# Norm, gate and merge of the sequence per chunk, two first projection tiles slice by slice, inverted blocks interleaved with their transpose

## The chip, the cores and the metric

The kernel runs on one core of a Trainium2 chip. The metric is the device time of one execution in microseconds. The core has five engines with queues of their own: TensorE (PE, matrix products, with weight loads listed as PEld), VectorE (DVE), ScalarE (ACT), GpSimd (POOL, hardly used here) and SyncE (SP, which only issues transfers here). ScalarE issues transfers too (ACTq in the trace), and while it does, it computes nothing.

## What is computed

Two layers of a hybrid decoder, for a prompt of 256 tokens and 8 sample tokens, 264 in all, with a model width of 1024. Each layer has three sublayers: a feed-forward half step, the mixing, and a second feed-forward half step. Cut to what matters:

```python
x = sub_out(x, swiglu(sub_in(x, 0), ffn_up[0], ffn_down[0]), 0, 0.5)
h = sub_in(x, 1)
pa, pb, pg = split_cols(h @ w_in, [A_COLS, B_COLS, 2 * D_MODEL])
ya = rwkv7_branch(pa, ...)            # sequential state update, 16 heads of 64
yb = gdn_branch(pb, ...)              # gated DeltaNet, 8 heads of 128, chunks of 64 tokens
g_a, g_b = jnp.split(jax.nn.sigmoid(pg), 2, axis=-1)
x = sub_out(x, (g_a * ya + g_b * yb) @ w_out, 1, 1.0)
x = sub_out(x, swiglu(sub_in(x, 2), ffn_up[1], ffn_down[1]), 2, 0.5)
...
# gdn_branch, per chunk of 64 tokens
tinv = triangular_solve(eye + L, eye)                 # one 64x64 inverse per head and chunk
v_new = u_c - w_c @ S;  o = q_c @ S + a_c @ v_new;  S = S * exp(gl_c) + k_c.T @ v_new
...
o = o * rsqrt(mean(o * o, axis=-1) + 1e-6) * norm_w   # per head: over its 128 columns
o = o * silu(z)
```

The shift, scale and gate of each sublayer come from a conditioning vector by a product with w_ada.

## The kernel before

**Tiles and the weight stream.** Activations are kept feature-major, 128 partitions by 8 slices by 264 tokens. A weight tile is 128 output columns by 8 slices, 512 KB in fp32. SyncE loads the tiles, in the order of a plan that is written at the start (a list of keys), into a ring of five slots. ScalarE casts each tile to fp32r (`w_hi`, L718), VectorE makes the rest (`ring_r`, L726), and TensorE multiplies each slice three times: high by high, high by low, low by high (`linear`, L860), 24 matmuls a tile. A helper `ahead` has both make a tile two tiles before TensorE uses it. Conditioning tiles (`w_ada`) are in the same plan. They are used in pieces of four matmuls (`ada_piece`); during the mixing they all go through one slot of the ring, the fifth.

**Entries.** The first projection tile of a sublayer waits slice by slice for its activation (`entering`, `h_ready`), which ScalarE and VectorE make one slice after another.

**Mixing.** It has 76 turns (`TURNS`), in each of which `dense(t)` multiplies one tile of w_in. Every other part of the mixing hangs on turn numbers at the top of the file (L56 to L63), and the same turn loop is written for each engine, so the order on a queue is the order of this loop. The triangular inverses are made three times a layer (`run` 0, 1 for the RWKV branch, 2 for the gated DeltaNet) for 16 units of 128 rows at a time: `gather` (8 transfers from SBUF to DRAM, L563) and `fetch` bring the 16x16 diagonal blocks side by side, `solve` inverts them on VectorE, `store` writes the result and its transpose (L578), `clear` zeroes the target on ScalarE (L608, L609, L611), `scatter` issues 16 transfers of 16 KB from ScalarE that lay the blocks on the diagonals (L620), and `invert` joins the blocks to 32 and 64 by four steps of 64 or 128 small matmuls (L639, L647, L652), with VectorE between them. `invert` waits for all transfers of `scatter`; in the other direction the scatter waits for the clear.

**Tail.** After the last turn comes the gated DeltaNet over four chunks: on TensorE `attend(c)` and the state, on VectorE the new state and values. The output of a chunk lies in PSUM bank 4 and ScalarE copies it to `y` (L1774). Sample steps and reads of the sample states (`sample_reads`) are laid between the chunks. Only after the last chunk come the norm (ScalarE squares a head, TensorE sums it with `ones_all`, ScalarE makes logarithm and exponential, L1378 and L1380), six VectorE operations for the head (L2322 to L2335), and this for eight heads one after another. The out projection waits for all eight (`merged`). Behind the merge ScalarE issues loads of sample states.

Of the kernel before, what the change touches and what calls it, by code (L numbers as in the profile page):

```python
# [19 lines left out]
P = 128  # L20
DEPTH, D = 2, 1024
NT = D // P
# [34 lines left out]
PREP0, CONV0, SEQ0, MOUT, LAST_AT = 5, 28, 40, 52, 53  # L57
UNIT0, ROWS0, HEAD0, GN0, SAMP0, SILU0 = 53, 53, 56, 61, 64, 70
# [3 lines left out]
GATHER0, FETCH0, SOLVE0, STORE0 = (18, 30, 65), (19, 31, 66), (20, 32, 67), (22, 34, 69)  # L62
CLEAR0, SCATTER0, INV0 = (29, 34, 67), (30, 35, 70), (31, 36, 71)  # L63
# [72 lines left out]
def weight_plan():  # L136
# [3 lines left out]
    for l in range(DEPTH):  # L140
# [14 lines left out]
        for t in range(TURNS):  # L155
            plan.append((l, *TILES[t]))
# [36 lines left out]
def build(nc, I, O):  # L193
    ctx = ExitStack()
    with ctx:
# [108 lines left out]
        def g_bv4(hf, cp, g):  # L304
# [5 lines left out]
        t_blocks = nc.dram_tensor("t_blocks", [2, P, B16, B16], F32, kind="Internal").ap()  # L310
        solve_bufs = [[qk[:, 21 + n, 3:3 + NPR] for n in range(3)] + [qk[:, 20, 3:3 + NPR]]] * 2
        solve_bufs += [[pa[:, NT + n, 0:NPR] for n in range(4)]]
        inv_sets = [(g_lt if n == 2 else prod_b[:, UNITS * n:UNITS * (n + 1), C:2 * C], part(big, inv_t_at[n], UNITS, C),
                     part(big, inv_t_at[n] + 1024, UNITS, C), part(big, inv_x_at[n], UNITS, C)) for n in range(3)]
# [10 lines left out]
        p_tmp = part(big, NT * T, 4, T)  # L325
# [212 lines left out]

        INV_PE = 5
# [32 lines left out]
        def store(act, run):  # L572

            act.wait_ge(solved.sem, solved.at(run + 1))
            if run:
                act.wait_ge(block_out.sem, block_out.at(18 * run))
            for n in range(2):
                act.dma_start(t_blocks[n, :, :, :], square(solve_bufs[run][1 + n])).then_inc(block_out.sem, block_out.one())  # L578

        def solve(dve, run, half):  # L580

            got, t_blk, tt_blk, prod = solve_bufs[run]
            got, t_m = square(got), square(t_blk)
# [5 lines left out]
            if half == 0:  # L589
                if run == 1:  # L590
                    dve.wait_ge(block_out.sem, block_out.at(18))
                dve.wait_ge(block_in.sem, block_in.at(9 * (run + 1)))
                after(dve.tensor_scalar(t_m, got.rearrange("p s t -> p t s"), -1.0, None, ALU.mult))
                dve.memset(t_blk[:, 0:NPR:B16 + 1], 1.0)
# [6 lines left out]
            if half == 1:  # L601
                dve.tensor_copy(square(tt_blk), t_m.rearrange("p t s -> p s t")).then_inc(solved.sem, solved.one())

        def clear(act, run):

            lt, t_b, tt_b, x_b = inv_sets[run]
            zero = bm(ident64[:, :], UNITS)
            act.mul(t_b, zero, 0.0)  # L608
            i = act.mul(tt_b, zero, 0.0)  # L609
            if run != 1:  # L610
                i = act.mul(x_b, zero, 0.0)  # L611
            i.then_inc(inv_z.sem, inv_z.one())

        def scatter(act, run):

            act.wait_ge(inv_z.sem, inv_z.at(run + 1))
            act.wait_ge(block_out.sem, block_out.at(18 * run + 2))
            for n, into in enumerate(inv_sets[run][1:3]):
                for rows, cols, part_of in blocks():
                    act.dma_start(into[rows, :, cols], t_blocks[n, part_of, :, :].rearrange("u s t -> s u t")).then_inc(block_out.sem, block_out.one())  # L620

        def invert(pe, run, s):

            lt, t_b, tt_b, x_b = inv_sets[run]
            n = 4 + s // 2
            if s == 0:

                pe.wait_ge(block_out.sem, block_out.at(18 * (run + 1)))
# [7 lines left out]
            if s % 2 == 0:  # L636
                for u in range(UNITS):
                    for hf in HALVES:
                        i = pe.matmul(banks[2][hf, u * 32:(u + 1) * 32].rearrange("p (a t) -> p a t", t=1 << n), lt[hf, u, :],  # L639
                                      unit_cols(t_b[hf, u, :], n, 0), start=True, stop=True)  # L640
# [3 lines left out]
            if n < 5:  # L644
                for u in range(UNITS):
                    for hf in HALVES:
                        i = pe.matmul(banks[4][hf, u * 32:(u + 1) * 32].rearrange("p (a t) -> p a t", t=1 << n), tt_b[hf, u, :],  # L647
# [1755 lines left out]
```

## Time and profile before

| what | us |
|---|---|
| median of three runs | 2300.95 (2300.72 to 2302.95) |
| profiled execution | 2309.99 |
| its span in the trace | 2308.3 |
| TensorE busy | 2076.7 (90%) |
| VectorE busy | 1269.5 (55%) |
| ScalarE busy | 958.1 (42%) |
| mean DMA rate | 153 GB/s |

Durations come from the one profiled execution, which was a little slower than the median run. "Busy" leaves out the issuing of transfers, so ScalarE is occupied longer than its 42%. PEclk is the granted clock of TensorE as a share of full speed. A wait is idle time of an engine just before an instruction, put down to the instruction that ended it.

### The profile page before, as it was taken

Reading aid. Unit: us, or ns where it says so; the run is one execution under the profiler, and the core shown is the slowest. Engines: PE = TensorE matmul, PEld = TensorE weight load, DVE = VectorE, ACT = ScalarE, POOL = GpSimd, SP = SyncE. Lnnn points to the kernel's source line nnn. Section 1 sums busy time; section 2 is a strip of 40 time slices with the busy share of each in tenths; the row PEclk is TensorE's granted clock in tenths of the full one; section 3 lists DMA queues with packets and bytes.
Section 4 is the critical chain, followed back from the end, with each engine's and each line's share of the span. In section 5 each row is a group of like instructions: output and inputs, shape, how many; then the busy total and the mean of one; then the engine's idle time right before and its main releaser. Section 6 shows DMA issues by size and latency. Waiting matters only on the chain.

```text
span 2308.3 us, 44992 instructions
## 1 busy us (share of the span) xinstructions
PE 2076.7 (90%) x19116; PEld 1863.6 (81%) x19116; DVE 1269.5 (55%) x2227; ACT 958.1 (42%) x1890; POOL 4.8 (0%) x30
## 2 busy tenths in 40 slices
PE   6999898989989896899989998988798988779997
PEld 4899777878878875788989996877797877569997
DVE  3454445654466256577556644464554744658863
ACT  3343553434475304423454445333345642153343
POOL 0000000000000000000000000000000000000000
PEclk7999999989999867899999999889899987689999
DMA  7877555555555615587646664444344444237863
GB/s 244 227 223 209 153 168 164 147 143 142 145 140 148 159 46 128 151 240 228 192 124 181 177 176 135 119 122 111 89 117 125 110 116 121 71 101 211 231 195 95
DMA packets 593718, 353.35 MB, mean 153 GB/s; under 512 B 57140, under 2 KB 554326, under 8 KB 591966
## 3 DMA queue, kind: packets, MB, share of 16 engines
q1 hardware_dynamic: 489344, 302.23, 45.9%
q10 hardware_dynamic: 104174, 48.25, 8.7%
q8 instruction: 151, 2.47, 0.5%
q14 instruction: 49, 0.40, 0.1%
HBM read 332.27 MB, written 18.50 MB: 152 GB/s over the span
## 4 chain that ended last, share of the span: by engine, by line
PE 73%; DVE 9%; DMA 6%; ACT 5%; ACTq 4%; issue 3%; SPq 0%; DVEq 0%
PE bank L858 70%; DMA ring<-in_w_ada 3%; ACTq L620 2%; DVE ring_r L726 1%; DMA ring<-in_ffn_up 1%; PE bank L639 1%; ACT w_hi_r L718 1%; DVE big L1838 1%; DVE far L1838 1%; PE bank L652 1%; DMA far<-t_blocks 1%; DVE y L1841 1%; DVE h L1838 1%; DVE y L1838 1%; PE bank L647 1%
## 5 line engine op out<-in xcount | busy, mean ns | idle before, releaser
L858 PE MATMUL bank<-big_r,w_hi_r 128*128 128x264 f32 x4160 | 1091.4, 297 | 49.7 <-DVE h_r L1838 37.6
L858 PE MATMUL bank<-big_r,ring_r 128*128 128x264 f32 (+1 forms) x3456 | 1004.1, 291 | 0.0
L858 PEld LDWEIGHTS bank<-big_r,w_hi_r 128*128 128x128 f32 x4160 | 758.1, 194 | 126.8 <-issue 94.9
L858 PE MATMUL bank<-h_r,w_hi_r 128*128 128x264 f32 x2752 | 807.7, 293 | 0.0
L726 DVE TENSOR_TENSOR ring_r<-ring,w_hi_r 128x1024 fp32r<-128x1024 f32 (+2 forms) x440 | 524.2, 1195 | 464.9 <-ACT w_hi_r L718 461.2
L858 PEld LDWEIGHTS bank<-big_r,ring_r 128*128 128x128 f32 (+1 forms) x3456 | 673.7, 195 | 1.0
L718 ACT CAST w_hi_r<-ring 128x1024 fp32r<-128x1024 f32 (+2 forms) x440 | 452.8, 1030 | 480.5 <-PE bank L858 291.7
L858 PEld LDWEIGHTS bank<-h_r,w_hi_r 128*128 128x128 f32 x2752 | 541.4, 197 | 1.1
L858 PE MATMUL bank<-big,far 64*64 64x64 f32 (+2 forms) x1440 | 159.1, 266 | 0.0
L858 PEld LDWEIGHTS bank<-big,far 64*64 64x64 f32 (+1 forms) x1440 | 124.5, 144 | 7.6 <-issue 7.1
L858 PE MATMUL bank<-ring,c 128*32 128x256 f32 x1152 | 96.4, 415 | 20.9 <-DMA ring<-in_w_ada 15.6
L1838 DVE TENSOR_TENSOR big<-big,bank 128x264 f32<-128x264 f32 (+3 forms) x144 | 66.4, 468 | 72.2 <-PE bank L858 60.1
L858 PE MATMUL bank<-big 128*64 128x64 f32 (+5 forms) x608 | 81.6, 299 | 16.0 <-DVE big L1838 14.4
L858 PE MATMUL bank<-far 64*64 64x64 f32 (+2 forms) x928 | 89.1, 255 | 1.1 <-ACT far L1497 1.1
L858 PEld LDWEIGHTS bank<-big 128*64 128x64 f32 (+2 forms) x608 | 60.8, 181 | 34.0 <-DVE big L1838 19.1
L858 PEld LDWEIGHTS bank<-far 64*64 64x64 f32 (+2 forms) x928 | 64.8, 145 | 15.7 <-issue 12.7
L1841 DVE SCALAR_TENSOR_TENSOR rs<-big,pcol,rs 128x256 f32<-128x256 f32 x78 | 37.8, 485 | 58.2 <-ACT rs L1542 56.0
L639 PE MATMUL bank<-far 64*64 64x32 f32 x768 | 34.1, 256 | 37.5 <-DMA far<-t_blocks 37.5
L858 PE MATMUL bank<-far,big 64*64 64x64 f32 (+1 forms) x576 | 67.7, 255 | 0.0
L639 PEld LDWEIGHTS bank<-far 64*64 64x64 f32 x768 | 32.6, 178 | 39.6 <-DMA far<-t_blocks 38.8
L858 PEld LDWEIGHTS bank<-ring,c 128*32 128x32 f32 x1152 | 24.5, 112 | 47.4 <-DMA ring<-in_w_ada 23.4
L858 PEld LDWEIGHTS bank<-far,big 64*64 64x64 f32 (+1 forms) x576 | 57.5, 162 | 6.0
(288 smaller groups left out, 1981.5 us busy)
## 6 DMA issues: line engine op xcount, KB each, us to landing
ring<-in_ffn_up SPq DMA_DIRECT2D x176, 512.0 KB, 4.3
ring<-in_w_in SPq DMA_DIRECT2D x148, 512.0 KB, 3.8
ring<-in_w_ada SPq DMA_DIRECT2D x144, 512.0 KB, 4.1
ring<-in_ffn_down SPq DMA_DIRECT2D x64, 512.0 KB, 3.8
far<-in_state_gdn_ssm ACTq DMA_DIRECT2D x28, 512.0 KB, 5.4
ring<-in_ffn_down SPq DMA_DIRECT2D x32, 384.0 KB, 3.2
ring<-in_w_out SPq DMA_DIRECT2D x16, 512.0 KB, 3.8
out_sample_gdn_ssm<-far ACTq DMA_DIRECT2D x16, 512.0 KB, 4.2
```

Source lines behind the costliest of these rows:

```text
L620: act.dma_start(into[rows, :, cols], t_blocks[n, part_of, :, :].rearrange("u s t -> s u t")).then_inc(block_out.sem, block_out.one())
L639: i = pe.matmul(banks[2][hf, u * 32:(u + 1) * 32].rearrange("p (a t) -> p a t", t=1 << n), lt[hf, u, :], unit_cols(t_b[hf, u, :], n, 0), s ...
L647: i = pe.matmul(banks[4][hf, u * 32:(u + 1) * 32].rearrange("p (a t) -> p a t", t=1 << n), tt_b[hf, u, :], unit_cols(x_b[hf, u, :], n, 0), ...
L652: i = pe.matmul(banks[3][hf, u * 32:(u + 1) * 32].rearrange("p (a t) -> p a t", t=1 << n), x_b[hf, u, :], unit_cols(tt_b[hf, u, :], n, 1), ...
L718: act.copy(w_hi[:, m % HI, 0:size], ring[:, slot[n], 0:size]).then_inc(hi_ready.sem, hi_ready.one())
L726: dve.tensor_tensor(ring_r[:, slot[n], 0:size], w, w_hi[:, m % HI, 0:size].bitcast(F32), ALU.subtract).then_inc(lo_ready.sem, lo_ready.one())
L858: return pe.matmul(out, lhsT, rhs, start=start, stop=stop)
L1838: return dve.tensor_tensor(out, a, b, op)
L1841: return dve.scalar_tensor_tensor(out, a, s, b, op0, op1)
```

## The change

There are three parts.

1. The inverted blocks and their transposes are held in one array whose last dimension is 2 (block value, transposed value). So there is one store and there are 8 scatters of 16x16x32 elements instead of 16 of 16x16x16, the clear is two operations, and the operands of `invert` are read at a step of two floats. The turn numbers move: there is one turn more between scatter and inversion, and what depends on the inverses (`SEQ0` and the constants behind it) comes two turns later.
2. `enter` multiplies the first two tiles of a sublayer's projection slice by slice together, at all six entries. In the mixing the plan has both tiles ahead of the first two conditioning tiles.
3. Norm, silu gate, branch gates and merge of the gated DeltaNet are made per chunk (64 tokens, all eight heads at once, 512 columns) during the chunk sequence, and the sample reads move ahead of the chunks. The branch gates and the conditioning operations move to the head of the tail.

```diff
-PREP0, CONV0, SEQ0, MOUT, LAST_AT = 5, 28, 40, 52, 53
-UNIT0, ROWS0, HEAD0, GN0, SAMP0, SILU0 = 53, 53, 56, 61, 64, 70
+PREP0, CONV0, SEQ0, MOUT, LAST_AT = 5, 28, 42, 54, 55
+UNIT0, ROWS0, HEAD0, GN0, SAMP0, SILU0 = 55, 55, 58, 63, 66, 72
-GATHER0, FETCH0, SOLVE0, STORE0 = (18, 30, 65), (19, 31, 66), (20, 32, 67), (22, 34, 69)
-CLEAR0, SCATTER0, INV0 = (29, 34, 67), (30, 35, 70), (31, 36, 71)
+GATHER0, FETCH0, SOLVE0, STORE0 = (18, 30, 66), (19, 31, 67), (20, 32, 68), (22, 34, 69)
+CLEAR0, SCATTER0, INV0 = (29, 35, 67), (30, 36, 70), (32, 38, 72)
...
         def scatter(act, run):
...
-            for n, into in enumerate(inv_sets[run][1:3]):
-                for rows, cols, part_of in blocks():
-                    act.dma_start(into[rows, :, cols], t_blocks[n, part_of, :, :].rearrange("u s t -> s u t")).then_inc(block_out.sem, block_out.one())
+            into = inv_sets[run][1].rearrange("p u t w -> p u (t w)")
+            for rows, cols, part_of in blocks():
+                act.dma_start(into[rows, :, 2 * cols.start:2 * cols.stop], t_blocks[part_of].rearrange("u s t w -> s u (t w)")).then_inc(block_out.sem, block_out.one())
...
+                    def enter(outs, keys, x_hi):
+
+                        both = [weights((l, *key)) for key in keys]
+                        for k in range(NT):
+                            pe.wait_ge(h_ready.sem, h_ready.next(pe))
+                            for out, (hi, lo) in zip(outs, both):
+                                mm(out, hi[:, k, :], x_hi[:, k, :], k == 0, False)
+                                mm(out, hi[:, k, :], h_lo[:, k, :], False, False)
+                                i = mm(out, lo[:, k, :], x_hi[:, k, :], False, k == NT - 1)
...
+                    def post_sum(c):
+
+                        pe.wait_ge(post_sq.sem, post_sq.at(c + 1))
...
+                        mm(bank, ones_all[:, :], square.rearrange("p n t -> p (n t)")).then_inc(post_ss.sem, post_ss.one())
...
                     for c in range(1, NC):
+                        first, *others = ((0, 1), (2, 3, 4), (5, 6, 7))[c - 1]
+                        sample_reads(first)
+                        post_sum(c - 1)
+                        for n in others:
+                            sample_reads(n)
...
+                    def post_square(c, bank):
...
+                        act.activation(post_t[c][1], src, ACT.Square).then_inc(post_sq.sem, post_sq.one())
+                        return act.copy(y[:, :, post_cols[c]], src)
...
+                    for c in range(NC + 1):
+                        post_cut(c)
...
+                    act.wait_ge(merged.sem, merged.at(NC + 1))
                     load_samples(samp_both, sa_in)
...
+                    def post(c):
+
+                        dve.wait_ge(post_rs.sem, post_rs.at(c + 1))
+                        yc = y[:, :, post_cols[c]]
+                        settle(stt(yc, yc, g_nw, post_t[c][0], ALU.mult, ALU.mult))
+                        settle(tt(yc, yc, zs[:, :, post_cols[c]]))
+                        tt(yc, yc, pa[:, 0:NT, post_cols[c]], ALU.add).then_inc(scaled.sem, scaled.one())
+
+                    def post_low(c):
+                        dve.wait_ge(cut_ready.sem, cut_ready.next(dve))
+                        tt(h_lo[:, :, post_cols[c]], y[:, :, post_cols[c]], hi_out[:, :, post_cols[c]].bitcast(F32), ALU.subtract).then_inc(merged.sem, merged.one())
```

On ScalarE, turn 30, the first run's scatter; `far` is the SBUF array that holds the target and `lt_blocks` the gather of the next run. Before:

```order
L1368 COPY modv<-bank7 128x36
L718 CAST w_hi_r<-ring 128x1024
L1486 COPY big<-bank0 128x264
L1487 COPY svx<-bank0 128x11
L620 DMA far<-t_blocks 16x16x16 x16
L563 DMA lt_blocks<-far 16x16x16 x8
L1547 ACTIVATE big<-svx 128x256
L1542 ACTIVATE rs<-big,pcol 128x256
L718 CAST w_hi_r<-ring 128x1024
```

The same place of the change:

```order
L1402 COPY modv<-bank7 128x36
L723 CAST w_hi_r<-ring 128x1024
L1520 COPY big<-bank0 128x264
L1521 COPY svx<-bank0 128x11
L625 DMA far<-t_blocks 16x16x32 x8
L570 DMA lt_blocks<-far 16x16x16 x8
L1581 ACTIVATE big<-svx 128x256
L1576 ACTIVATE rs<-big,pcol 128x256
L723 CAST w_hi_r<-ring 128x1024
```

The sequence around it is the same; the scatter is half as many transfers, each twice as large, and the gather still stands behind it.

On TensorE, the end of the first layer's tail, from the last chunk's output (bank 4) to the out projection (bank 0). Before, with the two remaining sample reads (`cva`), one bridge per sample step (bank 7), and the eight norm sums:

```order
L858 MATMUL bank4<-big 128x64
L858 MATMUL bank4<-far,big 128x64
L858 MATMUL bank2<-far,cva 16x128 x8
L858 MATMUL bank7<-ident64,svx 64x64 x2
L858 MATMUL bank2<-far,cva 16x128 x8
L858 MATMUL bank7<-big,centre 128x64
L858 MATMUL bank3<-ysel,far 128x32 x2
L858 MATMUL bank7<-rs,ones_half 128x64
L858 MATMUL bank4<-big,ones_all 128x264
L858 MATMUL bank5<-big,ones_all 128x264
...
L858 MATMUL bank0<-big_r,w_hi_r 128x264
```

The change:

```order
L863 MATMUL bank4<-big 128x64
L863 MATMUL bank4<-far,big 128x64
L863 MATMUL bank2<-ysel,far 128x32 x2
L863 MATMUL bank7<-ident64,svx 64x64 x2
L863 MATMUL bank3<-far,ones_all 128x512
L863 MATMUL bank7<-big,centre 128x64
L863 MATMUL bank1<-far,ones_all 128x64
L863 MATMUL bank7<-rs,ones_half 128x64
L863 MATMUL bank0<-big_r,w_hi_r 128x264
```

Both sample reads and eight sums have left this stretch; one sum of 512 columns and one of 64 are in it. The other three sums and the reads stand between the chunks.

On TensorE, the entry of the mixing in the first layer; bank 0 and bank 1 take the first two tiles, `ring,c32` is a conditioning piece. Before, one place ahead of the second tile and one behind it:

```order
L858 MATMUL bank0<-big_r,ring_r 128x264
L858 MATMUL bank7<-ring,c32 32x256 x4
L858 MATMUL bank1<-big_r,w_hi_r 128x264
L858 MATMUL bank1<-h_r,w_hi_r 128x264
...
L858 MATMUL bank1<-big_r,ring_r 128x264
L858 MATMUL bank7<-ring,c32 32x256 x4
L858 MATMUL bank0<-big_r,w_hi_r 128x264
```

The change, the last slice of both tiles and what follows:

```order
L863 MATMUL bank0<-big_r,ring_r 128x264
L863 MATMUL bank1<-big_r,w_hi_r 128x264
L863 MATMUL bank1<-h_r,w_hi_r 128x264
L863 MATMUL bank1<-big_r,ring_r 128x264
L863 MATMUL bank7<-ring,c32 32x256 x8
L863 MATMUL bank0<-big_r,w_hi_r 128x264
```

The tiles alternate by slice, and the two conditioning pieces, which had a whole tile between them, stand back to back.

## Rows read from the trace of the kernel before

**Rows 1.** The page, busy time and share of TensorE, weight loads and other engines.

```profile
PE 2076.7 (90%) x19116; PEld 1863.6 (81%) x19116; DVE 1269.5 (55%) x2227; ACT 958.1 (42%) x1890; POOL 4.8 (0%) x30
```

**Rows 2.** The waits of TensorE: us in total, times, longest us.

```profile
PE bank L858 <- DVE h_r L1838: 37.6, 8, 8.2
PE bank L639 <- DMA far<-t_blocks: 37.5, 6, 9.9
...
PE bank L858 <- ACT big L1813: 25.2, 16, 1.9
```

**Rows 3.** Timeline of ScalarE, first inversion: start, us, engine, line, what, count.

```profile
474.51 1.33 ACTq L620 DMA_DIRECT2D far<-t_blocks  x3
...
475.87 6.47 ACTq L620 DMA_DIRECT2D far<-t_blocks  x13
482.44 4.65 ACTq L563 DMA_DIRECT2D lt_blocks<-far  x8
```

**Rows 4.** Timeline of TensorE, first inversion, its steps 0 and 2.

```profile
484.14 3.62 PE L639 MATMUL bank<-far 64*64 64x32 f32 x64 [5.93 <-DMA far<-t_blocks]
...
500.59 2.06 PE L639 MATMUL bank<-far 64*64 64x32 f32 x64
```

**Rows 5.** Windows: length, busy (count) of PE, PEld, DVE, ACT, POOL, clock, DMA, GB/s.

```profile
484.10:490.10 6.00, 5.96 (x78) 5.08 (x79) 2.04 (x4) 2.67 (x7) 0.00 (x0) 0.50 0.28 46
788.50:868.60 80.10, 74.91 (x501) 62.65 (x501) 38.15 (x41) 7.18 (x12) 0.00 (x0) 0.72 0.35 86
...
898.40:928.40 30.00, 29.92 (x208) 29.05 (x208) 10.03 (x9) 14.22 (x33) 0.00 (x0) 0.90 0.71 193
```

**Rows 6.** Timeline of ScalarE and of TensorE, second inversion of layer 1.

```profile
1646.97 1.94 ACTq L620 DMA_DIRECT2D far<-t_blocks  x2
...
1657.33 3.63 PE L639 MATMUL bank<-far 64*64 64x32 f32 x64 [9.92 <-DMA far<-t_blocks]
```

**Rows 7.** Timeline of ScalarE, end of the first layer's tail.

```profile
862.66 0.59 ACT L1774 COPY y<-bank 128x512 f32<-128x512 f32 x1 [19.23 <-PE bank L858]
...
875.15 0.48 ACT L1378 ACTIVATE big<-bank,epsc 128x264 f32<-128x264 f32 x1 [1.40 <-PE bank L858]
...
898.47 2.37 ACTq L1823 DMA_DIRECT2D far<-in_state_gdn_ssm  x3
```

**Rows 8.** Timeline of TensorE, end of the first layer's tail.

```profile
866.48 2.15 PE L858 MATMUL bank<-far,cva 128*16 128x128 f32 x16
...
873.80 1.25 PE L858 MATMUL bank<-big,ones_all 128*128 128x264 f32 x2 [1.85 <-ACT big L1813]
...
898.43 0.59 PE L858 MATMUL bank<-big_r,w_hi_r 128*128 128x264 f32 x1 [3.88 <-DVE h_r L1838]
```

**Rows 9.** Timeline of VectorE, head and end of the first layer's tail.

```profile
796.80 0.69 DVE L2216 COPY big<-bank 128x512 f32<-128x512 f32 x1 [8.99 <-PE bank L858]
...
870.93 2.35 DVE L1838 TENSOR_TENSOR far<-far,delta 128x1024 f32<-128x1024 f32 x2
...
876.85 0.49 DVE L1841 SCALAR_TENSOR_TENSOR y<-y,pcol,far 128x264 f32<-128x264 f32 x1
```

**Rows 10.** Timeline of TensorE, entry of the first mixing.

```profile
284.04 0.56 PE L858 MATMUL bank<-big_r,w_hi_r 128*128 128x264 f32 x1 [4.32 <-DVE h_r L1838]
284.39 0.42 PE L858 MATMUL bank<-h_r,w_hi_r 128*128 128x264 f32 x1
284.61 0.42 PE L858 MATMUL bank<-big_r,ring_r 128*128 128x264 f32 x1
...
290.32 0.64 PE L858 MATMUL bank<-ring,c 128*32 128x256 f32 x8
290.89 0.39 PE L858 MATMUL bank<-big_r,w_hi_r 128*128 128x264 f32 x1
...
295.75 0.64 PE L858 MATMUL bank<-ring,c 128*32 128x256 f32 x8 [1.69 <-DMA ring<-in_w_ada]
```

More of the change, by code:

```diff
@@ L324, in build @@
         vnx = part(big, gt + 1024, 2, NS, HD_B)
-        p_tmp = part(big, NT * T, 4, T)
+        post_cols = [slice(c * C, (c + 1) * C) for c in range(NC)] + [slice(NPR, T)]
+        post_t = [(part(big, WORK, NT, C), part(big, WORK + 512, NT, C))] * NC + [(part(big, WORK + 1024, NT, NS), part(big, WORK + 1088, NT, NS))]
         gs_kept = [part(big, ZG + 1024 * n, NS, HD_B) for n in range(3)]
@@ L537, in level_bank, with pair_cols @@
             return banks[bank][:, :].rearrange("p (u a t) -> p u a t", u=UNITS, t=1 << n)
+        def pair_cols(both, n, w, side, u=None):
+            cols = "p u (a h t) -> p u a h t" if n == 4 else "p u (h a t) -> p u a h t"
+            v = both[:, :, :, w].rearrange(cols, h=2, t=B16)[:, :, :, side, :]
+            return v if u is None else v[:, u]
         INV_PE = 5
@@ L575, in store @@
             if run:
-                act.wait_ge(block_out.sem, block_out.at(18 * run))
-            for n in range(2):
-                act.dma_start(t_blocks[n, :, :, :], square(solve_bufs[run][1 + n])).then_inc(block_out.sem, block_out.one())
+                act.wait_ge(block_out.sem, block_out.at(9 * run))
+            act.dma_start(t_blocks[:, :, :, :], solve_bufs[run][1]).then_inc(block_out.sem, block_out.one())
         def solve(dve, run, half):
-            got, t_blk, tt_blk, prod = solve_bufs[run]
-            got, t_m = square(got), square(t_blk)
+            got, both, prod = solve_bufs[run]
+            got, t_m = square(got), both[:, :, :, 0]
             def after(i):
@@ L601, in solve @@
             if half == 1:
-                dve.tensor_copy(square(tt_blk), t_m.rearrange("p t s -> p s t")).then_inc(solved.sem, solved.one())
+                dve.tensor_copy(both[:, :, :, 1], t_m.rearrange("p t s -> p s t")).then_inc(solved.sem, solved.one())
         def clear(act, run):
[L606 to L609, printed above, removed]
+            lt, both, x_b = inv_sets[run]
+            zero = bm(ident64[:, :], 2 * UNITS)
+            i = act.mul(both.rearrange("p u (a t) w -> p (u a) (t w)", a=2), zero, 0.0)
             if run != 1:
-                i = act.mul(x_b, zero, 0.0)
+                i = act.mul(x_b, bm(ident64[:, :], UNITS), 0.0)
             i.then_inc(inv_z.sem, inv_z.one())
@@ L858, in mm, with weights @@
                         return pe.matmul(out, lhsT, rhs, start=start, stop=stop)
-                    def linear(out, key, x_hi, x_lo, start=True, stop=True, entering=False):
-                        key = (l, *key)
+                    def weights(key):
                         m, n = split_no[key], where[key]
@@ L865, in linear @@
                         pe.wait_ge(lo_ready.sem, lo_ready.nth(m + 1))
[L866 to L867 removed]
+                        return (w_hi[:, m % HI, 0:kt * cols].rearrange("p (k n) -> p k n", k=kt),
+                                ring_r[:, slot[n], 0:kt * cols].rearrange("p (k n) -> p k n", k=kt))
+                    def linear(out, key, x_hi, x_lo, start=True, stop=True):
+                        hi, lo = weights((l, *key))
+                        kt = tile_size(*key)[0]
                         for k in range(kt):
[L869 to L870 removed]
                             mm(out, hi[:, k, :], x_hi[:, k, :], start and k == 0, False)
@@ L975, in dense @@
                         if k < 2:
-                            pe.wait_ge(out_taken.sem, out_taken.at(NT))
+                            if k == 0:
+                                pe.wait_ge(out_taken.sem, out_taken.at(NT))
+                                enter([banks[g][:, 0:T] for g in range(2)], TILES[0:2], hi_in)
+                            return
                         elif k - 2 < A_TILES:
@@ L1708, in _ @@
                         for run in range(3):
-                            if t == GATHER0[run]:
+                            if t == GATHER0[run] and run < 2:
                                 gather(act, run)
@@ L1712, in _ @@
                                 fetch(act, run)
-                            if t == STORE0[run]:
+                            if t == STORE0[run] and run < 2:
                                 store(act, run)
```

229 lines of the change are left out of this document (116 added, 113 removed).

## The prediction

> **What bounds the kernel now.** I read the page first: TensorE has work in 2076.7 of 2308.3 us [rows 1], a share of 90%. So time comes back where TensorE waits, or where it runs at the lower clock after a wait. VectorE and ScalarE matter only where TensorE waits for them. The list of TensorE's waits comes next [rows 2]: 37.6 us for the low part of an activation (eight places, two of them at the out projections), 37.5 us in six waits for the scattered inverse blocks, 25.2 us in 16 waits for the squares of the post norm. The change touches all three.
>
> The six waits. There are three inversions in a layer. ScalarE issues 16 scatters for one, about 0.50 us each (13 in 6.47) [rows 3]. In the first, the last issue ends at 482.34 and TensorE starts at 484.14, after 5.93 us of nothing; the 64 small matmuls behind it take 3.62 us, and the same kind takes 2.06 us at 500.59 [rows 4]. The granted clock in the six us after the wait is 0.50 of full, the 1.2 GHz level [rows 5]. So a wait costs more than itself. The longest wait is 9.92 us, in layer 1 [rows 6].
>
> The post norm. Behind the last chunk's copy at 862.66 [rows 7] TensorE has eight squares to sum, each behind a 1.5 us wait on ScalarE, and the out projection starts only at 898.43, 3.88 us after it had nothing more [rows 8]. Between them stand, head by head, the square, the sum, a logarithm, an exponential and six VectorE operations, such as the one of 0.49 us [rows 9], all in a row.
>
> **The change, part by part.** The sum is against the profiled execution: 2309.99 us, of which the trace spans 2308.3. That run is 9.04 us over the median of 2300.95, and I carry this difference along.
>
> *Inversion.* Removed: 8 of 16 scatter issues (4.0 us of ScalarE's queue), one of two stores, one of three clears. Added: one more turn between scatter and first inversion matmul (30 to 32, 36 to 38, 70 to 72; before one turn less in each). For the first run: the scatter starts at 474.51 or a little later, eight issues with the work between them end near 479.2, and 2.3 us later (484.14 less the start of the last issue, 481.86) the blocks lie near 481.1. TensorE stood ready at 484.14 - 5.93 = 478.21. The turn that now comes first is a projection tile, 24 matmuls in 3.17 us (290.89 to 295.75 - 1.69 [rows 10]) and in most turns a conditioning piece of 0.64: 3.6 us and more, so 481.8 or later. No wait is left, but the margin is 0.7 us only. For the longest wait TensorE was ready at 1657.33 - 9.92 = 1647.41 and the scatter began at 1646.97 [rows 6]: with eight issues it lands about 7.1 us on, TensorE comes after 4.5, and some 2.5 us stay. I take 35.0 of 37.5 us as gone. Clock: five of the six blocks return 3.62 - 2.06 = 1.56, which is 7.8. The tile behind each block has its matmuls 0.22 apart where it takes 0.13 at full clock [rows 10]; over 24 that is 2.2 if the clock stays low for the whole tile, and I take 1.5, times five 7.5. Together 50.3. Against it, what moves in: the turn that TensorE now computes meets casts and copies that still queue behind eight scatter and, in the first run, eight gather issues (4.65 us [rows 3]) on ScalarE. Before, ScalarE's next work could begin at 482.44 + 4.65 = 487.1; with four us less it is 483.1, its cast and VectorE's low part end near 486.2, and TensorE needs them at about 484. I give it 2.3 us in all, since it can show in two of the six. **Minus 48.** Bounds: if the moved turn is worth nothing, the waits shrink by the 4.0 us of issues alone, 24 and some clock, minus 27. If all waits go and the small stalls of the neighbouring turns with them, minus 58.
>
> *Operands two words apart.* T and its transpose now alternate, so moving data and one kind of weights are read at a step of two floats. No row shows this. From below nothing. From above, that each group of 64 falls from 2.06 to the 3.62 us [rows 4] of half speed: 5 groups in a run, 30 in all, 1.56 more each, 47 us. The pace of the group follows TensorE's clock now (3.62 against 2.06), so the array bounds it, and a slower read counts only beyond that; I take 0. The Trainium skill speaks to it in SBUF — State Buffer, section Door 1: The DMA port swizzle, in its note on cachelines: a 16-byte line wants at least two hits, so fp32 at a step of two, two hits a line, should run at full rate; by that the sum stays, by the half-speed bound it would be 2276. No row here shows it either way, and the sum doesn't use it.
>
> *Tail.* Per layer, 898.43 - 862.66 = 35.8 us now. In it remain: the square of the last chunk, 0.6 (as the copy, 128x512 [rows 7]); the sum on TensorE, 2.4 at the rate of 1.25 for 264 columns [rows 8]; logarithm and exponential, the first 0.48 for 264 columns [rows 7], so about 1.25 for both at 512; three VectorE operations at some 0.75 (0.69 for a copy of 512 [rows 9]), 2.2; the sample step and its merge, 2.3; the cut and the low parts, 3.1 (four at 0.7 and a small one). That is 11.9, and 0.4 for hand-overs: 12.3. The norms of chunks 0 to 2 go under the chunk sequence, where VectorE has 38.15 busy of 80.1 us [rows 5]; if that cover were gone they would cost about 2.2 us of VectorE a chunk. What is not hidden is TensorE's part: three sums of 512 columns, 1.5 each between the two clock levels, 4.5; and two sample reads of 2.15 [rows 8], which stood behind the last chunk and now stand ahead, 4.3. So 35.8 - 12.3 - 4.5 - 4.3 = 14.7, times two 29.4. The large gate operations move to the head of the tail, where VectorE idles 8.99 us before the first copy of u [rows 9]; two of 2.35 us (2048 elements [rows 9]) and four small ones fit. **Minus 28**, with 0.7 a layer for hand-overs inside the sequence. Bounds: minus 22, where each sum takes the full 2.4 us and a hand-over, and minus 34, where the sums and reads hide in waits that TensorE has there anyway. Four loads of 512 KB more now go out after the merge, ahead of the cast of the third out tile: before 3 took 2.37 us [rows 7], seven take 5.5. The cast comes at about 904, TensorE needs it after two tiles, 48 matmuls at 0.22, 909. Hidden; next to be late would be the tile loads themselves.
>
> *Entries.* Six entries now run two tiles slice by slice. Now tile 0 takes from 284.04 to 290.32, 6.28 us or 0.79 a slice, where its matmuls need 3 x 0.22 = 0.66; tile 0, the piece and tile 1 end at 294.06, 10.0 us after the start [rows 10]. Interleaved: the clock rose after six us, so 27 of 48 matmuls at 0.22, then 21 at 0.13, 8.7 us, against 9.4 without the piece: 0.7 gained at most, and in the four feed-forward entries the third tile's cast and low part wait behind the table load, so I put 0.5 each there, minus 2. In the two mixing entries both conditioning pieces now follow the two tiles, and they share one slot of the ring: the second load starts only when the first piece is read. It came 295.75 - 290.96 = 4.8 us after the first piece, of which 1.69 were a wait [rows 10]. Now nothing lies between them and two tile loads go ahead of it: 4.8 to 6.0 of waiting, 3.1 to 4.3 more, less 0.7. **Plus 6** for two, **plus 4** with the others. Bounds plus 1 and plus 8.
>
> Sum: -48 - 28 + 4 = -72. Profiled execution 2238, median 2300.95 - 72 = 2229. With the bounds: -27 - 22 + 8 = -41 to -58 - 34 + 1 = -91.
>
> **Rivals.**
> (a) The waits of the inversion only change hands. TensorE gets to the moved turn and stands there for ScalarE, which is still issuing, or the half clock stays since it falls for other gaps nearby. For it: the 0.7 us margin above, and ScalarE's queue of issues, which is blocked for 4.65 us more by the gathers behind the first [rows 3]. Against it: 4 us of issue are truly gone. Then -16 - 28 + 4: 2261, or little above.
> (b) The other side: strided reads are slow. It decides at 72 / 30 = 2.4 us more for each group of 64, 2.06 to 4.5. At three times the duration, 4.1 x 30 = 124, the result is 2353. Against it: that the array's clock sets the pace now. With the half-speed price of 47 it is 2276, still faster.
> (c) Transfers collide after the merge. Near 898 to 928 the DMA share is 0.71 at 193 GB/s, 5.8 MB in 30 us [rows 5]; 2 MB more need 10 us at this rate, and if half of it holds up the tiles: +5 a layer, 2239.
> (d) Everything goes at its upper bound: 2210.
> (e) The change does nothing measurable: the waits reappear in full and the tail's gain is eaten by the entries and the sums inside the sequence. It needs two independent failures.
>
> **Chances.** The forecast with its bounds, (c) within it: 0.73. (a) 0.10. (d) and beyond 0.08. (b) 0.05, of which 0.03 slower, and 0.02 for a slowdown of another kind. (e) 0.02. The range reaches from just under (d) to (a): 2207 to 2262. This kernel's measurement tells no change apart from 0.2%, 4.6 us. Faster 0.93, same 0.02, slower 0.05.
>
> **What would show it.** The six waits at the inversion's first matmuls should be near zero in the list of waits, their blocks of 64 at 2.1 us; if the blocks take 3.6 after no wait, operands are slow. ScalarE's scatters should be 48, the last issue some 4 us after the first. From the last chunk's square to the first out-projection matmul 12 to 13 us. The conditioning waits should grow by 6 us or so at the two mixing entries. The prediction is wrong if TensorE's waits for ScalarE's casts or VectorE's low parts grow by 15 us or more, if the chunk sequence (80.1 us now) grows by more than 12, or if the out projection stalls on its tiles.

## The result and the profile after

The changed kernel takes 2271.5 us (median of four runs, 2266.79 to 2278.63), the kernel before 2301.95 in the same comparison. The ratio is 0.9869, with a 95% interval of 0.9842 to 0.9897: 24 to 36 us faster, where 72 were forecast and 39 was the least that the range held.

The page of the changed kernel: span, busy time, and the chain that ended last by line.

```profile
span 2270.3 us, 44806 instructions
...
PE 2062.6 (91%) x19104; PEld 1854.5 (82%) x19104; DVE 1257.5 (55%) x2161; ACT 954.2 (42%) x1872; POOL 4.8 (0%) x30
...
PE bank L863 71%; DMA ring<-in_w_ada 3%; DVE ring_r L731 2%; DVE far L1888 1%; ACT w_hi_r L723 1%; DVE big L1888 1%; PE bank L657 1%; PE bank L644 1%; ACTq L1873 1%; DMA ring<-in_ffn_up 1%; ACTq L625 1%; ACTq L570 1%; DVE big L1891 1%; DVE far L1891 1%; PE bank L652 0%
```

Its waits of TensorE, in us in total, times, longest:

```profile
PE bank L863 <- DVE h_r L1888: 42.2, 8, 8.2
...
PE bank L863 <- DMA ring<-in_w_ada: 33.4, 21, 6.3
PE bank L863 <- DVE ring_r L731: 19.2, 7, 7.3
...
PE bank L644 <- DMA far<-t_blocks: 5.6, 2, 2.8
```

Against [rows 2]: the wait for scattered blocks fell from 37.5 to 5.6 us, the one for the squares of the post norm (25.2) is gone. Two others grew. Conditioning tiles cost 15.6 us in 16 waits before and cost 33.4 in 21 now; low parts of weight tiles (`ring_r`) cost 5.4 us before and 19.2 now. These two, 31.6 us together, are most of what is missing.

The largest of the first kind is at the entries of the mixing; one is in each layer. It answers to the last of [rows 10]. Timeline of TensorE:

```profile
299.16 1.08 PE L863 MATMUL bank<-ring,c 128*32 128x256 f32 x8 [6.17 <-DMA ring<-in_w_ada]
```

The second kind is in the out projection. Timeline of ScalarE behind the last chunk of layer 0, answering to [rows 7]:

```profile
867.73 0.60 ACT L1814 ACTIVATE far<-bank 128x512 f32<-128x512 f32 x1 [16.58 <-PE bank L863]
...
871.13 0.69 ACT L1412 ACTIVATE far<-bank,epsc 128x512 f32<-128x512 f32 x1 [1.78 <-PE bank L863]
871.85 0.63 ACT L1414 ACTIVATE far<-far 128x512 f32<-128x512 f32 x1
...
879.57 2.42 ACTq L1690 DMA_DIRECT2D far<-in_state_rwkv_wkv  x4
882.02 9.91 ACTq L1873 DMA_DIRECT2D far<-in_state_gdn_ssm  x3
892.03 1.04 ACT L723 CAST w_hi_r<-ring 128x1024 fp32r<-128x1024 f32 x1 [14.76 <-issue]
```

And TensorE in the same stretch, answering to [rows 8]:

```profile
869.02 2.07 PE L863 MATMUL bank<-far,ones_all 128*128 128x512 f32 x2
...
879.59 0.59 PE L863 MATMUL bank<-big_r,w_hi_r 128*128 128x264 f32 x1 [6.26 <-DVE h_r L1888]
...
894.39 0.59 PE L863 MATMUL bank<-big_r,w_hi_r 128*128 128x264 f32 x1 [7.30 <-DVE ring_r L731]
```

From the last square to the out projection it is 11.9 us (forecast 12.3). But the third out tile comes at 894.39. ScalarE makes its cast only at 892.03, because it issues seven loads of 512 KB first: four take 2.42 us, the three behind them 9.91, where three had taken 2.37 [rows 7]. The kernel before issued its four of these loads 29 us earlier than the three, at 869.46. It has such a slow issue too, at the head of the first tail, where ScalarE issues seven loads of 512 KB in a row; six take 5.7 us, the seventh 7.26:

```profile
791.36 3.08 ACTq L1762 DMA_DIRECT2D far<-in_state_gdn_ssm  x2
794.48 7.26 ACTq L1762 DMA_DIRECT2D big<-in_state_gdn_ssm  x1
```

### The profile page after: what moved, and what is told of

It reads as the page before. It is cut to its first block, busy times and chain, and to the rows that moved or that the text cites. A ratio compares the mean times of both kernels' runs of the same rounds, so it can differ in the third digit from the quotient of the medians.

```text
span 2270.3 us, 44806 instructions
## 1 busy us (share of the span) xinstructions
PE 2062.6 (91%) x19104; PEld 1854.5 (82%) x19104; DVE 1257.5 (55%) x2161; ACT 954.2 (42%) x1872; POOL 4.8 (0%) x30
## 4 chain that ended last, share of the span: by engine, by line
PE 74%; DVE 9%; DMA 6%; ACT 5%; ACTq 4%; issue 3%; SPq 0%; DVEq 0%
PE bank L863 71%; DMA ring<-in_w_ada 3%; DVE ring_r L731 2%; DVE far L1888 1%; ACT w_hi_r L723 1%; DVE big L1888 1%; PE bank L657 1%; PE bank L644 1%; ACTq L1873 1%; DMA ring<-in_ffn_up 1%; ACTq L625 1%; ACTq L570 1%; DVE big L1891 1%; DVE far L1891 1%; PE bank L652 0%
## 5 line engine op out<-in xcount | busy, mean ns | idle before, releaser
L863 PE MATMUL bank<-ring,c 128*32 128x256 f32 x1152 | 98.0, 420 | 36.7 <-DMA ring<-in_w_ada 33.4
L1888 DVE TENSOR_TENSOR big<-big,bank 128x264 f32<-128x264 f32 (+3 forms) x144 | 66.4, 468 | 87.0 <-PE bank L863 75.5
L1888 DVE TENSOR_TENSOR far<-bank,masks 128x512 f32<-128x512 f32 x32 | 20.6, 686 | 75.9 <-PE bank L863 75.9
L863 PE MATMUL bank<-ident,far 64*64 64x64 f32 (+1 forms) x608 | 60.4, 234 | 0.0
```

Source lines behind the costliest of these rows:

```text
L863: return pe.matmul(out, lhsT, rhs, start=start, stop=stop)
L1888: return dve.tensor_tensor(out, a, b, op)
```

## Experiments

All ratios are to the kernel before, with their 95% intervals. The difference in us is the ratio less one, times 2303. Where idle time and busy time of TensorE are given, they come from one profiled execution of each kernel.

**e1: three loads moved behind casts.**

```diff
-                    for n in range(3):
-                        act.dma_start(gs_kept[n], sample_state(I["state_gdn_ssm"][l], n)).then_inc(gk_in[n].sem, gk_in[n].one())
                     for o in range(NT):
                         ahead(act, high, (l, "out", o))
                         leave(o, banks[o % 4], ("out", o), 1, sq_out[:, o, :], 0.5)
+                        if 3 <= o < 6:
+                            act.dma_start(gs_kept[o - 3], sample_state(I["state_gdn_ssm"][l], o - 3)).then_inc(gk_in[o - 3].sem, gk_in[o - 3].one())
```

> The changed kernel, with the three loads of kept sample states issued by ScalarE after the casts of out tiles 3, 4 and 5 instead of right behind the merge. Theory A (issue queue): in the changed kernel these three issues took 9.91 us behind the four loads of 512 KB, so the cast of the third out tile was late and TensorE waited 7.30 and 6.16 us for its low part. With them moved both waits go, and the half clock behind them: 13 to 17 us under the changed kernel (2271.5), so 2255 to 2259; the wait of TensorE for VectorE's low parts falls from 19.2 to about 5 us. Theory B (bandwidth): the third tile itself comes late since 3.5 MB of sample states share the engines with the tiles; then the wait only changes its releaser to a transfer, and the gain is under 4 us.

Measured: 2255.95 us (0.9796, 0.9774 to 0.9817), 15.6 under the changed kernel. ScalarE in layer 0:

```profile
878.39 2.42 ACTq L1690 DMA_DIRECT2D far<-in_state_rwkv_wkv  x4
880.91 1.05 ACT L723 CAST w_hi_r<-ring 128x1024 fp32r<-128x1024 f32 x1 [4.81 <-issue]
...
892.60 0.46 ACTq L1876 DMA_DIRECT2D far<-in_state_gdn_ssm  x1
```

The cast is 2.5 us behind the start of the out projection (878.42), not 12.4, and an issue that comes ten us later takes 0.46 us again. The wait for low parts falls to 7.9 us. Theory A holds: the issuing engine was held up. The tiles are a little late as well, since in e1 a cast waits 2.02 us for a tile of w_out (at 892.49), but 7.9 us is not far above the 5.4 of the kernel before. TensorE's idle time fell by 8.4 us and its busy time by 8.6 (2062.6 to 2054.0), and from the second out projection to the end the mean granted clock is 0.96 where it was 0.95. So here the lower clock did go with the waits.

**e2, e3, e4: each part alone on the kernel before** (the parts of the diff as numbered under "The change").

> The kernel before with the inversion part alone (one interleaved array, eight scatters, turns moved). Theory A (the stamps of the changed kernel's trace): 28 to 32 us faster than before, since 32 us of waits for the scatters and the half clock behind them go, and 8 to 10 us come back as waits for conditioning tiles in turns that are shorter than such a load. Theory B (my sum): 44 to 50 us faster, the rest of the loss lies in the other parts.

> The kernel before with the tail part alone (norm, gates and merge per chunk, loads of sample states after the merge). Theory A: the stretch itself gains 14 to 19 us a layer as forecast and the out projection gives 7.6 to 8.6 back, net 14 to 19 us faster than before in all. Theory B: the stall in the out projection needs the other parts (the ring filled differently); then alone the tail gains 28 us or more.

> The kernel before with the entry part alone (first two tiles slice by slice at six entries, two conditioning pieces back to back at the two mixing entries). Theory A: 4 to 7 us slower: each mixing entry shows a wait of 6.2 us for the second conditioning tile where there were 1.69 and 2.04, and the four feed-forward entries gain nothing, since the third tile's low part sets the end. Theory B (my sum's feed-forward term): the feed-forward entries give 0.5 us each, so 3 to 4 us slower. Theory C: TensorE's clock rises sooner after an entry that has no gaps, and it comes out even or faster.

| kernel | median us | ratio (95%) | difference |
|---|---|---|---|
| e2 inversion alone | 2283.09 | 0.9919 (0.9901 to 0.9936) | -19 |
| e3 tail alone | 2285.17 | 0.9925 (0.9907 to 0.9943) | -17 |
| e4 entries alone | 2310.08 | 1.0028 (1.0010 to 1.0045) | +6 |

The product is 0.9872, the whole change measured 0.9869. So the parts add up, and each can be judged by itself. The inversion missed both theories, mine before the result (48) and the one read from the stamps afterwards (28 to 32): it is worth 19. The tail came out as Theory A said. The entries cost 2 to 10 us by the interval, which leaves room for Theories A and B and none for C.

Why 19? TensorE's waits in e2:

```profile
PE bank L862 <- DMA ring<-in_w_ada: 24.7, 24, 3.2
...
PE bank L643 <- DMA far<-t_blocks: 5.5, 2, 2.8
```

32.0 us of waits for blocks are gone, 9.1 came back for conditioning tiles. How the second came about stands in the queues of SyncE and TensorE, in layer 0 ahead of the second inversion:

```profile
510.07 0.37 SPq L846 DMA_DIRECT2D ring<-in_w_ada  x1
...
514.68 0.37 SPq L846 DMA_DIRECT2D ring<-in_w_ada  x1
```

```profile
509.37 0.64 PE L862 MATMUL bank<-ring,c 128*32 128x256 f32 x8
513.98 0.64 PE L862 MATMUL bank<-ring,c 128*32 128x256 f32 x8 [0.85 <-DMA ring<-in_w_ada]
520.00 0.64 PE L862 MATMUL bank<-ring,c 128*32 128x256 f32 x8 [2.27 <-DMA ring<-in_w_ada]
```

Each load goes out 0.06 us after the piece before it has been read (509.37 + 0.64 = 510.01), and the next piece waits until it lands.

The clock returned next to nothing. Windows over the mixing of layer 1 (from the fourth tile to the tail), the kernel before and then e2; length, busy of PE, PEld, DVE, ACT, POOL, clock, DMA, GB/s:

```profile
1424.70:1928.00 503.30, 449.78 (x5174) 405.92 (x5170) 261.35 (x557) 229.54 (x525) 0.00 (x0) 0.91 0.45 118
```

```profile
1413.50:1903.10 489.60, 450.93 (x5175) 405.13 (x5171) 261.64 (x558) 230.32 (x523) 0.00 (x0) 0.91 0.47 125
```

13.7 us less of length, 1.2 us more of busy time, the same mean granted clock. The sum had 1.56 us for each group and 1.5 for the tile behind it; for the three inversions of this layer, less the one at which TensorE is late, that would be 6 us of busy time less. The groups themselves did come back. All six first groups took 3.62 or 3.63 us before. In e2 three take 2.06, as the second does, and none more than 2.43, even behind a wait:

```profile
525.23 2.06 PE L643 MATMUL bank<-far 64*64 64x32 f32 x64
...
1605.49 2.43 PE L643 MATMUL bank<-far 64*64 64x32 f32 x64 [2.72 <-DMA far<-t_blocks]
```

That is 8.8 us for the six, a little more than the 7.8 in the sum. Over both mixings, from the entry to the out projection, TensorE is busy for 1086.9 us in e2 and was for 1088.2 before. So the rest of its work became slower by about as much. One such place is the first inversion, here in the changed kernel, TensorE:

```profile
488.42 0.64 PE L863 MATMUL bank<-ring,c 128*32 128x256 f32 x8 [2.01 <-DMA ring<-in_w_ada]
492.11 2.06 PE L644 MATMUL bank<-far 64*64 64x32 f32 x64
```

```profile
499.17 2.70 PE L652 MATMUL bank<-far 64*64 64x32 f32 x64 [1.32 <-DVE far L675]
501.68 3.60 PE L657 MATMUL bank<-far 64*64 64x32 f32 x64
505.21 1.08 PE L863 MATMUL bank<-ring,c 128*32 128x256 f32 x8
```

The first group comes without a wait and at 2.06 us, as forecast, with its operands two floats apart. A turn earlier stands a wait of 2.01 for a conditioning tile, and a turn later, behind a wait of 1.32 for VectorE, the lower level is back: 3.60 us for a group, 1.08 for a piece that takes 0.64 elsewhere. Here the slow stretch moved. Which wait brings it back at each of the other places wasn't tested. One trace can't show a few us of busy time: the stretch between the two mixings, which e2 leaves as it was, has 481.9 us of it before and 476.9 in e2. The timed runs help: idle time fell by 21.5 us and the kernel gained 15 to 23, which leaves next to nothing for the clock, and not 15.

**e5, e6: the two halves of the inversion part.** e5 has the interleaved array and the eight scatters with the turn numbers of before; e6 has the turn numbers of the change with two arrays and sixteen scatters. The core of e6 on the kernel before:

```diff
-GATHER0, FETCH0, SOLVE0, STORE0 = (18, 30, 65), (19, 31, 66), (20, 32, 67), (22, 34, 69)
-CLEAR0, SCATTER0, INV0 = (29, 34, 67), (30, 35, 70), (31, 36, 71)
+GATHER0, FETCH0, SOLVE0, STORE0 = (18, 30, 66), (19, 31, 67), (20, 32, 68), (22, 34, 69)
+CLEAR0, SCATTER0, INV0 = (29, 35, 67), (30, 36, 70), (32, 38, 72)
...
```

> The kernel before with one interleaved array and eight scatters, but all turn numbers as before. Theory A (a halved issue queue is worth its 4.0 us at each wait): the six waits for scattered blocks fall from 37.5 to 12 to 16 us, and since TensorE still waits there, the conditioning loads stay hidden behind these waits (15 to 17 us): 17 to 22 us faster than before, as much as with the turn moved. Theory B: the turn is what counts, and this gains under 10 us.

> The kernel before with the turn numbers of the change, but two arrays, sixteen scatters and three clears as before. Theory A: a moved turn gives TensorE 3.8 us or more of work before the blocks are needed; the six waits fall from 37.5 to 10 to 16 us, and 4 to 7 us come back as waits for conditioning tiles and for VectorE: 10 to 17 us faster than before. Theory B: without the shorter queue the moved tiles' casts stand behind 16 issues, and this gains under 6 us.

In e2 and e6 the turn numbers bring with them that ScalarE's silu and tanh operations share fewer turns and the third gather and store stand behind them.

e5: 2281.58 us, 0.9907 (0.9879 to 0.9934), -21, Theory A. e6: 2297.79 us, 0.9967 (0.9948 to 0.9985), -8, between its two theories. The shorter queue alone gives all that the whole part gives. The turn alone gives 8, and on top of the queue no gain shows. The waits, in e5 and then in e6:

```profile
PE bank L643 <- DMA far<-t_blocks: 18.8, 6, 6.1
PE bank L862 <- DMA ring<-in_w_ada: 18.7, 17, 2.0
```

```profile
PE bank L858 <- DMA ring<-in_w_ada: 27.0, 22, 2.9
...
PE bank L858 <- ACT big L1629: 13.5, 2, 8.0
PE bank L639 <- DMA far<-t_blocks: 12.4, 3, 5.4
```

Half of what e6 won is lost again in the middle row, which is 1.3 us in the kernel before. At the third inversion ScalarE issues sixteen scatters and only then makes the square of a group norm (L1629) for which TensorE waits 8.04 us at 755.21, and 5.42 in layer 1. ScalarE there:

```profile
745.15 8.71 ACTq L620 DMA_DIRECT2D far<-t_blocks  x16
```

In e2, with eight scatters, these waits are 1.0 and 1.1 us.

Blocks and conditioning together: 53.1 us in the kernel before, 37.5 in e5, 39.4 in e6, 30.2 in e2. The stretch from the first tile of the mixing to the out projection (difference of the starts of both in the timeline) tells the layers apart:

| kernel | layer 0 | layer 1 |
|---|---|---|
| before | 614.4 | 621.5 |
| e2, both halves | 608.0 | 605.1 |
| e5, no turn moved | 602.0 | 606.6 |
| e6, turn alone | 612.0 | 614.5 |

In layer 0 there is a conditioning piece in nearly every turn, in layer 1 in every second. In layer 0 the moved turn cost 6 us against e5, in layer 1 it gained 1.5. One profiled execution each; the timed ratios of e2 and e5 don't differ by more than their intervals. The timelines say where the conditioning waits of layer 0 come back: in e2 and in e6 5.3 and 5.8 us stand in turns 31, 36 and 37, at the inversions, and 2.2 in turns 43 and 52, which have other work since the sequence starts two turns later. e5 has none of the five. They come with the moved turns. In the kernel before, TensorE waited for the blocks in turns 31 and 36 (5.93 and 5.22 us), and no wait for a conditioning tile is near.

**e7, e8: the pieces of the mixing.** e7 takes the late loads of e1 and puts a projection tile between the first two pieces again; e8 also divides the five ring slots three to two instead of four to one.

```diff
     if l == 0:
-        return 1 if turn < 75 else 0
-    return 1 if turn % 2 == 0 or turn in (1, 3) else 0
+        return 1 if turn != 1 else 0
+    return 1 if turn % 2 == 0 or turn in (3, 5) else 0
```

and in e8 also

```diff
-            own = (RING - 1,) if kind == "ada" else range(RING - 1)
+            own = (RING - 2, RING - 1) if kind == "ada" else range(RING - 2)
```

> The changed kernel with the late loads of e1 and, in the mixing, no conditioning piece in turn 1 but one later (turn 75 in layer 0, turn 5 in layer 1), so that a projection tile lies between the first two pieces again. Theory A (one slot, one load at a time): the wait of 6.2 us at both mixing entries falls to some 2 us, 6 to 9 us faster than e1 (2256), so 2247 to 2250. Theory B: the load is late for another reason (tile loads ahead of it in the queue), and the wait only moves one turn on: within 2 us of e1.

> As e7, and in the mixing conditioning tiles have two slots of the ring and projection tiles three (before one and four). Theory A: the waits for conditioning tiles in layer 0 (14 to 15 us after the entry) come from one slot that is loaded only when it has been read; with two they fall under 4 us, and if three slots are enough for the projection tiles, 8 to 12 us faster than e7. Theory B: three slots are too few, and TensorE waits for low parts instead: no faster, or slower than e7.

e7: 2240.01 us (2236.66 to 2241.7), 0.9721 (0.9692 to 0.9750), the fastest kernel of the study, 16 us under e1 where 6 to 9 were expected. Its second piece, in TensorE's timeline:

```profile
291.37 0.64 PE L863 MATMUL bank<-ring,c 128*32 128x256 f32 x8
298.30 1.08 PE L863 MATMUL bank<-ring,c 128*32 128x256 f32 x8 [2.60 <-DMA ring<-in_w_ada]
```

The 6.2 us wait is 2.6. The entries account for 5.9 and 4.8 us (the start of the seventh tile of the mixing after that of the first, e7 against e1). The rest came further on in the mixing, where the later pieces now fall into other turns; why they fall better there wasn't tried.

e8: 2310.7 us, 1.0029 (1.0008 to 1.0050), 71 us over e7. Waits of TensorE in e8:

```profile
PE bank L863 <- DVE big L1888: 60.7, 30, 4.7
...
PE bank L863 <- DMA ring<-in_w_ada: 4.3, 4, 1.8
```

And of ScalarE's casts:

```profile
ACT w_hi_r L723 <- DMA ring<-in_w_in: 111.8, 61, 6.2
```

With two slots the conditioning wait is down to 4.3 us (20.3 in e7), which fits the single slot. It proves it less than the rows of e2 do, because the turns of e8 are longer and would hide a load better by themselves. Three slots are too few for the projection tiles: the casts wait 111.8 us for them (6.8 in e7). So it is slower, as Theory B said, but not by the wait that it named. TensorE's waits for low parts are 8.4 us (9.4 in e7); those for VectorE's other results (L1888) rise to 60.7 (35.2 in e7). All idle time together is 15.6 us more than in e7. The larger part of the loss is busy time, 2106.0 us for 2044.5, at a mean granted clock of 0.904 for 0.932.

**e9, e10, e11: what else e7 needs.** e9 is e7 with the turn numbers of before, e10 is e1 with all six entries as before, e11 is e7 with the four feed-forward entries as before (`enter` called with one tile, the second by `linear`).

> e7 with the turn numbers of the kernel before (interleaved array, eight scatters, per-chunk tail, late loads, pieces apart). Theory A: as in e5 against e2 the moved turn is worth nothing once the queue is half as long, and 0 to 5 us are won by leaving it: 2235 to 2240. Theory B: in e7 the conditioning waits are fewer, so the moved turn does pay there: 3 to 8 us slower than e7 (2240).

> The changed kernel with the late loads of e1 and all six entries as before (first tile alone, then the second; one piece between them in the mixing). Theory A (entries cost 6.4 us by e4): 5 to 8 us faster than e1 (2256), 2248 to 2251, so the slice by slice entry is worth 8 to 11 us once its pieces are apart (e7). Theory B (the gain of e7 over e1 is mostly where the other pieces fell): 2244 or less.

> e7 with the four feed-forward entries as before. Theory A (they gain nothing: the third tile's low part sets their end): within 2 us of e7 (2240). Theory B (my sum's 0.5 each, or more): 2 to 5 us slower than e7.

| kernel | median us | ratio (95%) |
|---|---|---|
| e9 | 2246.1 | 0.9741 (0.9713 to 0.9769) |
| e10 | 2249.65 | 0.9761 (0.9733 to 0.9789) |
| e11 | 2244.79 | 0.9736 (0.9707 to 0.9764) |

e9 and e11 don't differ from e7 by more than the intervals: neither theory of e9 or of e11 is shown wrong. By the medians the moved turn is worth 6 us there, but the intervals leave room for none. e10 is 6 us under e1, as the cost of the entries in e4 says. e7 is 0.4% under e10, at the edge of what the intervals tell: the slice by slice entry looks worth some 9 us once the pieces are apart, but e7 also moved the later pieces. How the 9 us divide between the mixing and the feed-forward entries, e11 is too noisy to say.

**e12: the tail alone with the late loads.**

> The kernel before with the tail part alone and the late loads of e1 (e3 with the three loads moved). Theory A (the stall of the out projection is all that the tail gives back): 13 to 17 us faster than e3, so 29 to 34 us faster than before, which is what the sum gave the tail (28). Theory B: the tail has another loss that e3's trace hides: under 26 us faster than before.

2270.47 us, 0.9847 (0.9825 to 0.9868), 35 us faster than before and 18 more than e3. TensorE's busy time is 7.9 us less than in e3 (2067.6 to 2059.7), its idle time 8.3. Theory A, a little over its upper end: the out projection's stall is, within the intervals, all that the tail gave back.

## Why the prediction was wrong

Of the 42 us that are missing, the inversion part accounts for 29, the tail for 11 and the entries for 2, by e2, e3 and e4.

**Inversion, minus 48: wrong, minus 19 to 21.** The first step held: 32 of 37.5 us of waits went (I took 35.0), and where TensorE is late in layer 1 two waits of 2.8 us stay (I took one of 2.5). Two steps failed.

The clock: "five of the six blocks return 1.56" and "I take 1.5, times five", 15.3 us together. The blocks did return 8.8 us, but other work took it up again, and the kernel as a whole got nothing that shows. I had priced the low clock as a cost of each wait that goes away with that wait. TensorE's busy time over the mixing of layer 1 was 449.78 us before and 450.93 in e2 at the same mean clock, though 15 us of waits had gone. In the first inversion of the changed kernel the lower level came back behind waits of 1.3 to 2.0 us; for the other places the cause stays open.

What moves in: "I give it 2.3 us in all". It was 9.1 us for conditioning tiles in the whole kernel, 8.2 of it in layer 0, and 1.4 for all other waits in sum. I had looked for ScalarE's casts in the moved turn, which were in time (low parts cost 5.9 us in e2, 5.4 before). The chain that I missed is the one slot through which all conditioning tiles go: read, load, read again takes about 4.8 us in [rows 10], and a light turn of TensorE takes 3.8. The rows of e2 show the chain, load behind read and read behind load. In the kernel before, the waits for blocks in turns 31 and 36 covered it; e5, which keeps these turns, keeps the cover (18.7 us of conditioning waits, against 24.7 in e2 and 27.0 in e6).

32.0 less 9.1 less 1.4 is 21.5 (TensorE's whole list of waits adds up to 223.0 us before and 201.5 in e2), which is within the interval of the measured part, 15 to 23. So rival (a) happened for the most part. It named the half clock that stays for other gaps nearby. It did not name the conditioning slot: it had TensorE wait for ScalarE's issues, which is what e6 shows with sixteen of them.

**Strided operands, 0: right.** The first group of 64 takes 2.06 us with interleaved operands. The half-speed bound (47 us) and rival (b) are out. The groups whose weights are read at this step (L652) take 2.11 us at full clock where they took 2.06, 0.05 more for 64 matmuls. The Trainium skill (SBUF — State Buffer, section Door 1: The DMA port swizzle) says in its note on cachelines that two hits on a 16-byte line are enough for full bandwidth; the moving operands agree, the weights but for these 0.05 us.

**Tail, minus 28: the sum right, its cover wrong, minus 17 measured.** The stretch to the out projection measured 11.9 us for 12.3, its terms 2.07 for the sum (2.4 in the sum), 0.69 and 0.63 for logarithm and exponential (1.25). The chunk sequence with its head grew from 61.5 to 70.6 us (801.19 to 862.66 before, 797.11 to 867.73 after), 9.1 for 9.5. e12, without the stall, is worth 35. What failed is the sentence "seven take 5.5. ... Hidden": seven took 12.3 us (2.42 and 9.91), since I took the duration of one issue from three at a quiet place and multiplied it. The trace of the kernel before had the row that speaks against it: seven in a row at the head of the tail took 13.0 us, the last alone 7.26. The cast was 7 us late in each layer, and the two waits of 7.30 and 6.16 us with the half clock behind them cost the 15.6 us that e1 took back. Rival (c) had the place right and named the wrong resource: the issuing engine was late, and the tiles only a little. Of the signs that the prediction set itself, low parts grew by 13.8 us (limit 15) and the chunk sequence by 9 (limit 12). Neither was passed, though the time fell outside the range: no sign had been set on the clock or on the single slot.

**Entries, plus 4: right in kind, plus 6 measured.** The two pieces waited 6.17 and 6.26 us, just over the 4.8 to 6.0 that I gave. For the feed-forward entries the 49th projection matmul comes on average 8.57 us after the first where it came at 8.98, so 0.4 each for my 0.5, too little for e11 to show. What is over comes from the two mixing entries.

The profiled execution of before (2309.99 us) was 4 to 8 us longer than the medians of the comparisons (2301.95 to 2306.3); stamps of single executions set against it therefore flatter each part. That is how I came to 28 to 32 for e2 after the result, when the timed ratio says 19.

## What to carry to other kernels

A wait that is removed uncovers whatever ran under it: before pricing it, list every periodic chain in the region (here one ring slot that is read, loaded and read again) and compare its period with the shortened turn. The price of a transfer's issue holds only for a burst as long as the one where it was read; work that an engine must do soon belongs ahead of a burst of issues, not behind it. Count a lower clock as regained only if nothing else in the region stops the engine. At the out projections it came back with the removed waits (8.6 us less busy time in e1, 7.9 in e12 against e3); in the mixing, with short waits all around, nothing came back that shows. Look at the busy time over the whole stretch, not at the one slow block.

## What was unexpected of the hardware

ScalarE issued four 512 KB loads in 2.42 us and the next three in 9.91 and 9.47 us (layers 0 and 1), 3.2 us each; in e1, ten us later, one took 0.46 again. In the kernel before six took 5.7 us and the seventh 7.26. Whether the number, the bytes or the time since the last one landed sets the point at which an issue becomes slow, no run here separates. A matmul's fp32 operands at a step of two floats cost nothing as moving data (2.06 us for 64 of 64x32, the same as contiguous) and 0.05 us in 64 as weights (2.11 for 2.06).
